# Chunks in halves by GpSimd in the mixer, glu and level heads, and the first norm's root behind its product

## The reference

```
for l in range(2):
    h = rmsnorm(x, norm_mix[l])
    u, q_lat, kv_lat, k_rope, hg_q, hg_f, hg_i, hg_g, gate_logits = split(h @ w_in[l])
    y_ssm = glu(gelu(s5_scan(u)) @ w_glu)           # y @ w_glu, z_out * sigmoid(z_gate)
    y_mla = attention(rmsnorm(q_lat) @ w_uq, rmsnorm(kv_lat) @ w_ukv, k_rope) @ w_o
    y_hg  = (rmsnorm(chunked_hgrn2(hg_q, hg_f, hg_i)) * silu(hg_g)) @ hg_w_o
    gates = sigmoid(gate_logits).reshape(256, 3, 1024)
    x = x + (gates0 * y_ssm + gates1 * y_mla + gates2 * y_hg) @ w_out[l]
    x = x + cross_attention(rmsnorm(x), rmsnorm(mem)); x = x + swiglu(rmsnorm(x))
```

## Time and profile before

| | |
|---|---|
| median of 3 runs | 1945.76 us (1945.71 to 1946.53) |
| profiled execution | 1944.08 us, its span 1942.2 us |
| TensorE busy | 1815.6 us (93%), 9937 matmuls |
| VectorE busy | 1195.3 us (62%) |
| ScalarE busy | 869.4 us (45%) |
| GpSimd busy | 234.3 us (12%) |
| DMA | 274.59 MB, mean 141 GB/s |

### The profile page before, as it was taken

The page is one execution under the profiler, slowest core; times in us unless marked ns, Lnnn a source line. Parts: engine busy times, 40 slices in busy tenths (PEclk is TensorE's granted clock), DMA queues, the critical chain, the costliest instruction groups (busy, mean ns, idle before and its releaser), DMA issues.

```text
span 1942.2 us, 26797 instructions
## 1 busy us (share of the span) xinstructions
PE 1815.6 (93%) x9937; PEld 1424.7 (73%) x9937; DVE 1195.3 (62%) x1871; ACT 869.4 (45%) x1417; POOL 234.3 (12%) x243
## 2 busy tenths in 40 slices
PE   7999998989999999999888999998899999889998
PEld 6675656669998865666477998656799864669986
DVE  6995745545667892754554566655477745546775
ACT  4224445354444412344455445345555543555553
POOL 4004213020000001414012000111200000130000
PEclk9999999999999999999999999999999999899999
DMA  5444442445565444445154666531365654135553
GB/s 157 129 137 141 131 139 99 141 114 174 157 186 179 125 128 138 140 133 172 32 166 121 191 185 189 145 100 66 113 180 164 195 153 119 55 104 166 167 190 133
DMA packets 192358, 274.59 MB, mean 141 GB/s; under 512 B 25616, under 2 KB 129540, under 8 KB 192228
## 3 DMA queue, kind: packets, MB, share of 16 engines
q1 hardware_dynamic: 191364, 269.86, 45.7%
q0 software_dynamic: 864, 3.02, 0.5%
HBM read 271.78 MB, written 1.05 MB: 140 GB/s over the span
## 4 chain that ended last, share of the span: by engine, by line
PE 81%; DVE 8%; ACT 5%; issue 3%; POOL 2%; DMA 0%; DVEq 0%; ACTq 0%; POOLq 0%
PE bank L398 43%; PE bank L396 28%; DVE WL L1146 2%; ACT WH L1414 2%; PE bank L662 1%; PE bank L583 1%; POOL WL L1146 1%; PE bank L1006 1%; PE bank L591 1%; PE bank L856 1%; ACT HTH L1414 1%; PE bank L486 1%; DVE bank L2063 1%; PE bank L709 1%; PE bank L633 1%
## 5 line engine op out<-in xcount | busy, mean ns | idle before, releaser
L1146 DVE TENSOR_TENSOR WL<-W,WH 128x1024 fp32r<-128x1024 f32 x288 | 352.9, 1225 | 226.9 <-ACT WH L1414 218.6
L1414 ACT ACTIVATE WH<-W 128x1024 fp32r<-128x1024 f32 x328 | 347.5, 1060 | 323.1 <-PE bank L398 251.4
L398 PE MATMUL bank<-HTH,WH 128*128 128x256 f32 x1536 | 439.4, 286 | 24.6 <-DVE WL L1146 14.7
L398 PE MATMUL bank<-HTH,WL 128*128 128x256 f32 x1536 | 435.2, 283 | 0.0
L398 PE MATMUL bank<-HTL,WH 128*128 128x256 f32 x1536 | 435.2, 283 | 0.0
L398 PEld LDWEIGHTS bank<-HTH,WH 128*128 128x128 f32 x1536 | 295.3, 192 | 31.3 <-DVE WL L1146 17.8
L398 PEld LDWEIGHTS bank<-HTL,WH 128*128 128x128 f32 x1536 | 295.4, 192 | 0.5 <-issue 0.5
L398 PEld LDWEIGHTS bank<-HTH,WL 128*128 128x128 f32 x1536 | 295.3, 192 | 0.0
L398 PE MATMUL bank<-WH,HTL 128*128 128x512 f32 x544 | 216.8, 398 | 0.0
L398 PE MATMUL bank<-WH,HTH 128*128 128x512 f32 x480 | 196.0, 408 | 15.6 <-POOL WL L1146 9.4
L398 PE MATMUL bank<-WL,HTH 128*128 128x512 f32 x480 | 191.2, 398 | 0.0
(11 more groups left out here) (408 smaller groups left out, 2405.5 us busy)
## 6 DMA issues: line engine op xcount, KB each, us to landing
W<-in_w_in SPq DMA_DIRECT2D x132, 512.0 KB, 3.7
W<-in_ffn_w_gate_up SPq DMA_DIRECT2D x176, 256.0 KB, 3.4
W<-in_w_up SPq DMA_DIRECT2D x176, 256.0 KB, 3.5
W<-in_ffn_w_down SPq DMA_DIRECT2D x44, 512.0 KB, 4.2
W<-in_w_down SPq DMA_DIRECT2D x44, 512.0 KB, 4.3
W<-in_w_out SPq DMA_DIRECT2D x32, 512.0 KB, 4.0
W<-in_ssm_w_glu SPq DMA_DIRECT2D x16, 512.0 KB, 3.7
W<-in_x_w_kv SPq DMA_DIRECT2D x16, 512.0 KB, 3.8
```

The costliest lines, as they stand in the source:

```text
L398: m = pe.matmul(out, at_a(a[x]), at_b(b[y]), start=(start and i == 0), stop=(stop and i == 2), skip_group_check=True)
L1146: eng.tensor_tensor(WL[:, m % HSLOTS, 0:width], W[:, n % RSLOTS, 0:width], h, ALU.subtract)\
L1414: copy = lambda dst, src, scale=1.0: act.activation(dst, src, ACT.Copy, scale=scale)
```

## The change

- `feature_steps` gets `halves` as `token_steps` had. The products hq, hi, hg, kv, ql, gates 0 to 5 take every second chunk in halves, split by GpSimd (`both_parts`). hf stays in float32. The activations' halves of only those four of eight row blocks that meet such chunks are made (`halves_of`), into the two halves of HTL (`half_slot`), right after the mix input is scaled; semaphore `mix_halves` ahead of hq.
- glu takes every second chunk in halves too; `glu_halves` ahead of it. Its activations' halves are made by GpSimd after the last gate's split.
- The level heads' product `yh` takes all four chunks in halves by GpSimd (`low="both"`). The heads' halves are made by ScalarE (`high_of`) and VectorE (`low_of`).
- GpSimd's program: all these splits come in the order of the chunks, around the latent root, the memory load and the memory norm's root.
- The first layer's norm is made as the second's: raw transposes of x, with the gain alone, root behind the product. For that SP loads norm_mix and the first chunk ahead of the other parameters, the parameters' transposes stand behind the first u, IDENT and the iotas come first on GpSimd, and the UT evictions move from ScalarE to VectorE.
- `token_row` broadcasts the root inside the matmul, without the copy RSR. In the FFN it stands one chunk earlier.

```
 TensorE
-            def feature_steps(tag, wname, l, act, K, c0, tiles, low="dve", kstep=2, extra=0):
+            def feature_steps(tag, wname, l, act, K, c0, tiles, low="dve", kstep=2, extra=0, halves=None):
...
+                    src, slot = act, lambda k: k
+                    if halves and k0 // kstep % 2:
+                        n, w = chunk(tag, rows(wname, l, k0, kstep, c0, cols), kstep, cols, "both")
+                        src, slot = halves, half_slot
...
-                pe.wait_ge(sem["rstd_rows"], rows_at[n])
+                pe.wait_ge(sem["rstd"], n + 1)
...
-                    m = pe.matmul(ps[:, tt * P:tt * P + P], RSR[:, tt, :], IDENT[:, :], start=(tt == 0),
+                    m = pe.matmul(ps[:, tt * P:tt * P + P], RSTD[:, n, tt:tt + 1].broadcast_to([P, P]), IDENT[:, :], start=(tt == 0),
...
                 if l == 0:
-                    norm_T(nrm)
+                    pe.wait_ge(sem["x_rows"], 16)
+                    for j in range(4):
+                        raw_T(nrm, j, None)
...
-                hf, hq = mixer_in("hf", 1824, 4), mixer_in("hq", 1312, 4)
+                hf, hq = mixer_in("hf", 1824, 4, halves=None), mixer_in("hq", 1312, 4)
...
-                if l:
-                    pe.wait_ge(sem["mix_scaled"], 1)
+                pe.wait_ge(sem["mix_scaled"], l + 1)
                 for _ in hf:
                     pass
+                pe.wait_ge(sem["mix_halves"], l + 1)
                 for _ in hq:
                     pass
...
                 pe.wait_ge(sem["y_ready"], 4 * (l + 1))
+                pe.wait_ge(sem["glu_halves"], l + 1)
                 glu(0)
...
-                token_out_wide(("yh", l), "hg_w_o", l, oHG, 4, low=None)
+                token_out_wide(("yh", l), "hg_w_o", l, oHG, 4, low="both")
...
-                            if (j, k0) == (1, 0):
+                            if (j, k0) == (0, KT - 2):
                                 token_row(n)
 GpSimd
+            def halves_of(dst, src, *ks):
+                pair = lambda t, k: t[:, k:k + 2, :].rearrange("p a b -> p (a b)")
+                for k in ks:
+                    high, low = pair(dst[0], half_slot(k)), pair(dst[1], half_slot(k))
+                    link(pool.tensor_copy(high, pair(src, k)))
+                    ins = pool.tensor_tensor(low, pair(src, k), high.bitcast(F32), ALU.subtract)
...
+                pool.wait_ge(sem["mix_scaled"], l + 1)
+                wait_full(pool, ("u", l, 3))
+                signal(halves_of(mix_half, HTF, 2, 6), "mix_halves", l + 1)
+                if l == 0:
+                    rope_angles(1)
+                split_to(split_before["ql", l, 1])
                 wait_freed(pool, ("lssq", l))
...
-                wait_full(pool, ("y", l, 3))
-                for k in range(2):
-                    part = lambda t: t[:, 4 * k:4 * k + 4, :].rearrange("p a b -> p (a b)")
-                    link(pool.tensor_copy(part(GTH), part(HTF)))
-                    ins = pool.tensor_tensor(part(HTL), part(HTF), part(GTH).bitcast(F32), ALU.subtract)
-                signal(ins, "gate_in", l + 1)
-                for m in range(split_before["gate", l, 1, 1], split_before["gate", l, 5, 1]):
-                    split_whole(m)
+                split_to(split_before["gate", l, 5, 1])
+                pool.wait_ge(sem["y_ready"], 4 * (l + 1))
+                signal(halves_of(glu_half, UT, 2), "glu_halves", l + 1)
+                split_to(split_before["glu", l, 0, 0, 1])
                 wait_full(pool, ("ho", l, 1))
                 load_mem()
+                split_to(split_before["glu", l, 1, 0, 1] + 2)
                 norm_rstd(nrm, halves=False)
 VectorE, first layer
-                    norm_rows(nrm, X)
-                    norm_cols(nrm, "norm_mix", l)
+                    for j in (1, 3):
+                        whole_cols(nrm, HTLF, mix_gain, j)
                     setup_states()
...
+                for _ in phases(l, 2 if l else 0):
+                    pass
+                wait_freed(dve, ("rb", nrm))
+                take_u(0)
+                take_u(1)
```

More of the change, by code:

```diff
@@ L478, in raw_T @@
             def raw_T(n, j, tag):
-                for tt in range(TT):
+                for tt in range(TT) if tag else ():
                     freed(*tag, tt, j // 2)
@@ L527, in feature_steps @@
                 for k0 in range(0, K, kstep):
-                    n, w = chunk(tag, rows(wname, l, k0, kstep, c0, cols), kstep, cols, low)
+                    src, slot = act, lambda k: k
+                    if halves and k0 // kstep % 2:
+                        n, w = chunk(tag, rows(wname, l, k0, kstep, c0, cols), kstep, cols, "both")
+                        src, slot = halves, half_slot
+                    else:
+                        n, w = chunk(tag, rows(wname, l, k0, kstep, c0, cols), kstep, cols, low)
                     need_rows(act, k0 + kstep)
@@ L689, in _, with mixer_in @@
                 nrm += 1
-                def mixer_in(name, c0, tiles, extra=0):
-                    return feature_steps((name, l), "w_in", l, HTF, KT, c0, tiles, low=None, extra=extra)
+                def mixer_in(name, c0, tiles, extra=0, halves=mix_half):
+                    return feature_steps((name, l), "w_in", l, HTF, KT, c0, tiles, low=None, extra=extra, halves=halves)
                 def mixer_tokens(name, c0):
-                    token_out((name, l), "w_in", l, HTF, KT, c0, 512, low=None)
+                    token_out((name, l), "w_in", l, HTF, KT, c0, 512, low=None, halves=mix_half)
                 def ssm_u(*qs):
-                    src = HTLF if l else HTF
+                    src = HTLF
                     ws = {}
@@ L1294, in rope_angles, with both_parts @@
                         last = pool.tensor_tensor(quarter, quarter, whole, ALU.subtract)
[L1295 removed]
+                        if tt < TT - 1:
                             link(last)
[L1297 removed]
+                signal(last, "rope_angles", i + 1)
             lows = [0]
[L1301 to L1308 removed]
+            def both_parts(m):
+                n, _ = splits[m]
                 width = chunks[n][2] * chunks[n][3]
@@ L1317, in split_whole, with split_to @@
                 signal(pool.tensor_tensor(low, raw, high.bitcast(F32), ALU.subtract), s, v)
-                lows[0] = m + 1
+            def split_to(upto):
+                for m in range(lows[0], min(upto, len(splits))):
+                    if splits[m][1] == "both":
+                        both_parts(m)
+                        lows[0] = m + 1
+                    else:
+                        low_parts(pool, "pool", lows, m + 1)
+            def halves_of(dst, src, *ks):
[4 more added lines that the diff above has]
+                    ins = pool.tensor_tensor(low, pair(src, k), high.bitcast(F32), ALU.subtract)
+                    if k != ks[-1]:
+                        link(ins)
+                return ins
             def load_mem():
@@ L1685, in _ @@
                     take_bu(l, 1)
-                else:
-                    for q in range(4):
-                        take_u(q)
                 if l == 0:
@@ L2339, in _ @@
-                    take_u(3)
+                    add_whole(nrm, HTLF, mix_gain, ("ffd", l - 1), RSTD[:, nrm - 1, :])
+                for _ in phases(l, 2 if l else 0):
[3 more added lines that the diff above has]
+                take_u(1)
+                for _ in phases(l, 3 if l else 1):
+                    pass
+                take_u(2)
+                for j in range(0, KT // 2, 2):
+                    wait_freed(dve, ("hT", nrm, j))
@@ L2340, in _ @@
+                for k in range(0, KT, 4):
+                    ins = tt_(HTF[:, k:k + 4, :], HTLF[:, k:k + 4, :],
+                              RB.rearrange("p (o t) -> p o t", o=1).broadcast_to([P, 4, S]), ALU.mult)
+                signal(ins, "mix_scaled", l + 1)
+                take_u(3)
+                if l == 0:
+                    setup_steps()
                 nrm += 1
@@ L2477, in _ @@
                 norm_rows(nrm, memX, memX)
+                for j in range(2):
+                    low_of(2 * j, 2, "hoT", l, j, dst=oHG)
                 norm_cols(nrm, "norm_mem", l)
```

217 lines of the change are left out of this document (109 added, 108 removed).

## The result

The changed kernel takes 1986.46 us (median of 4 runs, 1984.73 to 1987.18), the kernel before 1946.14 beside it: a ratio of 1.0214, 95% interval 1.0197 to 1.023. It is slower, as forecast, but by 40.3 us where 11.4 were forecast, and outside the range of 1933 to 1974. The direction of the forecast case was right and the size far too small.

The account below looks back on a forecast made before the run. TensorE, 81% of the chain that ended last, was taken as the bound. Gains of 33.9 us against losses of 45.3 made it 11.4 us slower than the 1945.76 median: 1957.2 us, range 1933 to 1974 for 8 in 10.

Parts of the forecast that it names:

- Work saved on TensorE, 27.2 us: Weight chunks multiplied in halves instead of float32 in mixer, gates, glu and level heads: 13.6 us gained per layer, 27.2 in all.
- Token row, 5.8: In the FFNs, the row one chunk earlier removes TensorE's waits for a low half: 5.8 us gained, bounds 3 and 9.
- Start, 0.9: Layer 0's first norm, root behind the product: 0.9 us gained, could be 0 or 1.6; GpSimd's work could eat it.
- The price of a split, 2.80 us: Each GpSimd split of a weight chunk beside VectorE's products holds VectorE for 0.72 + 2.08 = 2.80 us.
- Layer 0's waits, 19.3 + 4: Layer 0's mixer: TensorE waits 19.3 us for VectorE's states held by splits, then 4 more at the second level product.
- Layer 1's 13.6: Layer 1's mixer: TensorE waits 13.6 us in sum for VectorE's states, delayed by splits and the mix input's halves.
- Second glu and heads, 5.4: GpSimd's four splits delay the memory norm's root, and VectorE's low halves delay the heads' product: 2.7 us lost per layer.
- Clock, 3: Longer waits put TensorE partly at 1.2 GHz instead of 2.4: 0 to 8 us lost, taken as 3.
- The signs: Expected trace marks: TensorE waiting at y products, VectorE products up to 3.3 us, its idle gone, GpSimd busy some 370 us.
- VectorE is not held: Rival: a split costs VectorE under about 2.2 us, sum at zero; at 1 us or less, 1920 us. Chance 0.13.
- GpSimd itself is too slow: Rival: a split takes GpSimd 5.8 us, so TensorE waits for splits at some ten chunks: 1970 us. Chance 0.10.
- 3.39 us per split: By the skill page's letter a split holds VectorE its full 1.04 + 2.35 us; sum some 11 us higher in both layers.

Follow-up runs that it names:

- e8: Changed kernel with e6's GpSimd order, hq, kv, ql, hi, hg and heads' product in float32, mix input's halves made behind the third y product: 1922.15 us.
- e6: Changed kernel with the second glu's splits made before the heads' outputs, and the heads' splits behind the memory norm's root: 1966.14 us.

## Why the prediction was right in sign and short in size

- **Work saved on TensorE, 27.2 us: right as far as tested.** Of the new halves the fastest version (e8) has only those of gates 0 and 1 and of the glu, 11.2 us by the prediction's prices. TensorE's busy time there is 1804.2 us against 1815.6, 11.4 less, at nearly the same mean clock (0.981 and 0.982). No run isolates the other 16.0.
- **Token row, 5.8: right**, 6.8 in the profile alone and 9.1 between medians with an interval of about 3.
- **Start, 0.9: half right.** hf begins 1.1 us earlier, but VectorE's first states begin at 38.81 (38.70 before), since the mix halves do hold its small steps (1.14 us for 0.19 twice); with the halves moved away the states begin at 36.51 (e8). The prediction named this and priced it at nothing.
- **The price of a split, 2.80 us: right** (2.76 from the pair above, 2.74 to 2.78 for three of the four in the root's chain). Through layer 0's first two sets of states VectorE's instructions take 20.2 us more than their shortest, not 25.2 for nine splits: the two of kv, of 576 columns instead of 1024, cost some 1.4 each, and of the tenth, which comes only behind these states, nothing falls here.
- **Layer 0's waits, 19.3 + 4: near in sum** (20.6), **wrong in place**: at the y products they were 11.2 and 2.7 for some 8 and 11, the wait of 6.7 for the bank was missing, and the wait at the level products did not come. That the sum is near is partly luck. **Layer 1's 13.6: short by 6**, since the bank of the first y product had about 1 us of slack and was not examined; only the y products' own operands were.
- **Second glu and heads, 5.4: the failed step.** It priced what GpSimd's late root does to TensorE and put at nothing what four splits do to VectorE at that place: 15 small steps ahead of the one that frees a bank, held from 3.0 to 14.4 us. The waits there are 10.0 and 9.3 us, and with no split beside these steps 20.3 us came back (e6). Against a forecast gain of 1.5 us per layer, products included, the stretch grew by 11.7 and 12.4.
- **Clock, 3: far short.** By the prediction's prices products save 27.2 us; busy time fell by 7.2, so 20 us went into the lower clock. Most of it goes with the waits: e8, which has none of the new ones, is at 0.981. The start, with 2.3 us more of busy time and less waiting, is an exception, and no run changes the clock alone.
- **The signs**: TensorE's waits for y products, the held products of 3.3 us and the row without its wait came; GpSimd is busy for 400 us, not 370; VectorE's idle time ahead of the last y did not go: 10.2 of 15.9 us are left in layer 0 and 11.1 of 18.2 in layer 1, since TensorE itself was late by then. The waits for banks and in the second glu had no sign.
- The sum: 49.8 us more of idle TensorE, 27.2 less of work, 20.0 of clock: 42.6, the difference of the spans (the clock's term is what the other three leave). The rival "VectorE is not held" is refuted; "GpSimd itself is too slow" did not occur, for no wait of TensorE's mixers was for a split.

The Trainium skill (SBUF — State Buffer, "Who interferes with whom") says that whichever of two contending instructions of VectorE and GpSimd is first keeps the shared ports for its whole length while the other is blocked, and that a TENSOR_SCALAR can contend too, in a mode that uses both ports. The trace agrees in kind: the TENSOR_SCALAR of 128x8 at 278.74 takes 2.20 us, 0.17 in the kernel before, and ends 0.03 us after GpSimd's subtraction of 278.55. The 3.39 us per split that the prediction worked out from the page are the most that this rule allows, and they are not seen: the root's steps lose 0.72 and 2.04 us to a cast of 1.04 and a subtraction of 2.36, since GpSimd is already under way (by 0.19 us at 278.74) when VectorE's step comes up.

## What to carry to other kernels

Before work goes to GpSimd, list every chain of VectorE that it will stand beside, the short steps too: a chain of 0.17 us steps is held as long per split as one of 1.23 us products, and costs more in proportion. Ask of a late engine not only who waits for its results but who waits for what it empties, and then redo the queue of the engine that is late as a whole: here waits for one late engine didn't add, and removing one moved it. The same work can be cheap or dear by where it is queued: 20 us here for four splits per layer taken away from 15 small steps, two to before them and two to behind.

## What was not expected of the hardware

An instruction of VectorE on 8 numbers per partition is held by GpSimd as long as one on 1024: 0.17 us became 0.89 beside a cast and 2.23 beside a subtraction, 1.23 became 1.94 and 3.26. And waits of TensorE cost a second time, as clock: some 20 us beside 49.8 of idle time, by the sum above. It went away with them (mean granted clock 0.965 in the changed kernel, 0.981 in the fastest version, 0.982 before).
